# Out projection interleaved with the latent attention, 64-row scores and VectorE-released expert slots in a two-block transformer kernel

## The reference

```python
# block one, one layer
h, hc = rms_norm(x)*(1+mod1)+mod0, rms_norm(ctx)*(1+modc1)+modc0
qa, ka, va, qb, kb, vb, rb, gb, qn, kn, vn = split_in(h @ w_in)      # the same of hc
# ya: differential attention, 4 heads, softmax(q0 k0) - lam*softmax(q1 k1), 64 features each
# yb: gated linear attention; decay = log_sigmoid(gb @ w_dec + b_dec)/16, gb is 2 x 16 features
# yn: neighbourhood attention, 4 heads of 64 features
x = x + mod2 * (concat(ya, yb, yn) @ w_out)
x = x + mod5 * hier_moe(rms_norm(x)*(1+mod4)+mod3)
# block two, two layers
# ya: latent attention, 8 heads of 64+32 features, masked by chunks -> features 0..511
# yb: stick breaking attention, yc: pooling                         -> features 512..1023
x = x + concat(ya, yb, yc) @ w_out
x = x + hier_moe_2(rms_norm_2(x))        # top 2 of 32 experts, silu(h@gate)*(h@up) @ down
```

## Time and profile before

| what | value |
|---|---|
| median of 3 runs | 1709.47 us (1708.24 to 1713.54) |
| profiled execution, its own time | 1704.93 us |
| its span | 1703.1 us |
| TensorE busy | 1376.3 us (81%) |
| VectorE / ScalarE / GpSimd busy | 444.9 / 396.4 / 45.6 us |
| moved by DMA | 479.72 MB, mean 282 GB/s |
| mean granted TensorE clock | 0.92 of full speed |

### The profile page before, as it was taken

One profiled execution on the slowest core, in us unless ns is written; L12 is line 12 of the kernel. 1 busy time (PEld: TensorE's weight loads), 2 busy tenths in 40 slices (PEclk: granted clock), 3 DMA queues, 4 the chain that ended last, 5 costly groups with the idle time before them and its releaser, 6 DMA issues.

```text
span 1703.1 us, 31490 instructions
## 1 busy us (share of the span) xinstructions
PE 1376.3 (81%) x12314; PEld 726.0 (43%) x12315; DVE 444.9 (26%) x1355; ACT 396.4 (23%) x766; POOL 45.6 (3%) x85
## 2 busy tenths in 40 slices
PE   3899996879666776799969788977798887999775
PEld 2555463445333342355547444333337544444332
DVE  0102436642111111122233613211122524122112
ACT  1101214312111121122223411212122422222222
POOL 2000111100000000000000000000000000000000
PEclk9999968979989898899979889988899987999997
DMA  9968320168999999999893145999975314579994
GB/s 333 323 234 249 108 66 0 30 258 319 410 410 410 410 409 410 409 361 379 318 341 126 72 163 217 418 418 418 417 276 198 146 66 198 219 292 419 417 418 183
DMA packets 126112, 479.72 MB, mean 282 GB/s; under 512 B 9089, under 2 KB 19582, under 8 KB 109358
## 3 DMA queue, kind: packets, MB, share of 16 engines
q1 hardware_dynamic: 122496, 468.61, 70.3%
q0 software_dynamic: 2656, 8.81, 1.7%
q10 hardware_dynamic: 910, 1.59, 0.3%
HBM read 477.01 MB, written 1.97 MB: 281 GB/s over the span
## 4 chain that ended last, share of the span: by engine, by line
PE 54%; SPq 19%; DMA 12%; DVE 7%; issue 4%; ACT 2%; ACTq 0%; POOL 0%; DVEq 0%; PEldq 0%
SPq L489 19%; DMA store<-in_w_up 8%; PE psum L1037 6%; PE psum L1712 6%; PE psum L713 5%; PE psum L1014 4%; PE psum L1027 4%; PE psum L987 4%; PE psum L1048 3%; PE psum L1708 3%; PE psum L1055 2%; DMA store<-in_w_expert_down 2%; PE psum L1262 2%; PE psum L1274 2%; PE psum L593 1%
## 5 line engine op out<-in xcount | busy, mean ns | idle before, releaser
L1027 PE MATMUL psum<-store 128*32 128x256 f32 x2624 | 178.3, 412 | 69.6 <-DMA store<-in_w_expert_up 69.6
L1037 PE MATMUL psum<-store 128*32 128x256 f32 x2432 | 157.9, 417 | 41.9 <-DMA store<-in_w_up 41.7
L1179 DVE TENSOR_TENSOR store<-store,psum 128x128 f32<-128x128 f32 x79 | 22.7, 287 | 568.4 <-ACT store L1112 568.4
L1027 PEld LDWEIGHTS psum<-store 128*32 128x32 f32 x2624 | 78.9, 115 | 153.3 <-DMA store<-in_w_expert_up 101.6
L987 PE MATMUL psum<-xn,store 128*32 128x256 f32 (+1 forms) x992 | 129.5, 489 | 5.4 <-DVE store L1142 5.4
L1037 PEld LDWEIGHTS psum<-store 128*32 128x32 f32 x2432 | 92.3, 120 | 97.3 <-issue 64.8
L1014 PE MATMUL psum<-store 32*128 32x256 f32 (+1 forms) x992 | 128.6, 474 | 1.9 <-ACT store L1117 1.9
L1112 ACT ACT_TABLE_LOAD x79 | 101.4, 1283 | 49.0 <-issue 48.7
L1112 ACT ACTIVATE store<-psum 128x128 f32<-128x128 f32 x79 | 21.9, 277 | 342.0 <-PE psum L1027 192.2
L1712 PE MATMUL psum<-store 128*128 128x512 f32 x224 | 97.7, 593 | 0.0
L1014 PEld LDWEIGHTS psum<-store 32*128 32x128 f32 (+1 forms) x992 | 58.6, 190 | 75.5 <-issue 70.1
(11 more groups left out here) (324 smaller groups left out, 1505.3 us busy)
## 6 DMA issues: line engine op xcount, KB each, us to landing
store<-in_w_expert_up SPq DMA_DIRECT2D x128, 1024.0 KB, 18.3
store<-in_w_expert_down SPq DMA_DIRECT2D x64, 1024.0 KB, 18.4
store<-in_w_gate SPq DMA_DIRECT2D x64, 1024.0 KB, 18.8
store<-in_w_up SPq DMA_DIRECT2D x64, 1024.0 KB, 20.7
store<-in_w_down SPq DMA_DIRECT2D x64, 1024.0 KB, 22.1
store<-in_w_mod SPq DMA_DIRECT2D x12, 2048.0 KB, 14.7
store<-in_w_in SPq DMA_DIRECT2D x6, 2048.0 KB, 9.4
store<-in_w_out SPq DMA_DIRECT2D x6, 2048.0 KB, 16.7
```

The costliest lines, as they stand in the source:

```text
L1027: mm = pe.matmul(out_(j), chosen_rows(k, 0), wt[:, kk, :, j, :], start=(k == 0), stop=(k == KD - 1))
L1037: mm = pe.matmul(out_(j), chosen_rows(k, e), wt, start=(k == 0), stop=(k == KD - 1))
```

## The change

1. **Latent attention's banks** (`score_of`, `turned_of`, `values_of`). Both scores of an item share one bank (4 or 5), both transposes share bank 6, the values of even and odd pairs share bank 7. Banks 0 to 3 are free.
2. **Out projection in block two.** The 16 matmuls of j=1 are issued two at a time (`fill`) between the scores of i+2 and the transposes of i, for each of the 8 items; j=0 follows the attention. Block one keeps its order.
3. **64-row scores in block one.** The two score matmuls of an item read the 64 rows of head 2g and of head 2g+1 in place. `q_pad`, GpSimd's copies and `q_padded` are gone.
4. **Expert slots.** The first four slots of a round are counted in a new semaphore, `up_used`, which VectorE raises by 4 after `hid` of an expert's last round; TensorE raises `piece_used` by 2 for the two down slots at the end of the round. SP waits for the one or the other.
5. **`gb` and the decay inputs** are packed: four groups of 128 tokens in the four 32-column parts of the array, and then four groups of 32 rows. The small matrix `wdec` is loaded four times (8 DMAs on GpSimd's queue where 2 were). TensorE waits for 12 `mod_col` (VectorE) instead of 12 `mod_row` (ScalarE).

```diff
+UP = 4
+    def used(self, j):
+        return ("up_used", UP) if j < UP else ("piece_used", ROUND - UP)
+    def freed(self, r, j):
+        name, each = self.used(j)
+        return self.sems[name], self.base[name] + each * r + (j if j < UP else j - UP) + 1
...
-                        sp.wait_ge(sems["piece_used"], turn * RING + (stage.base + ROUND * i + j + 1))
+                        sem, count = stage.freed(i, j)
+                        sp.wait_ge(sem, turn * (TURN * stage.used(j)[1]) + count)
...
+        def score_of(kind, i):
+            if kind == "mla":
+                return ps[4 + i % 2].rearrange("p (m n) -> p m n", m=2)
+            return psum[:, 2 * (i % 2):2 * (i % 2) + 2, :]
+        def turned_of(kind, i, m):
+            if kind == "mla":
+                return ps[6][:, S * m:S * m + S]
+            return ps[4 + (i % 2 if kind == "diff" else m)]
+        def values_of(kind, g):
+            return ps[7][:, S * (g % 2):S * (g % 2) + S] if kind == "mla" else ps[6 + g % 2][:, 0:S]
...
-                if kind != "mla":
-                    pe.wait_ge(*at.plus("q_padded", i + 1))
...
-                        q, k = q_pad[:, i % 2, m, :], k_all[:, g, :]
+                        r = slice(64 * m, 64 * m + 64)
+                        q, k = (qnT if kind == "na" else qaT)[r, g, P * t:P * t + P], k_all[r, g, :]
...
-                if g >= 2:
-                    pe.wait_ge(*at.plus("pv_sb", g - 1))
+                lag = 1 if kind == "mla" else 2
+                if g >= lag:
+                    pe.wait_ge(*at.plus("pv_sb", g + 1 - lag))
...
                     scores(i + 2)
+                if fill:
+                    fill(i)
                 turns(i)
...
+        def out_steps_pe(pe, slot, j, first, last):
+            w = piece_at(slot, 4 * D).rearrange("p (k n) -> p k n", k=4)
+            for step in range(first, last):
+                t, n, k = step // 8, step // 4 % 2, step % 4
+                mm = pe.matmul(ps[2 * t + n], mixT[:, 4 * j + k, P * t:P * t + P], w[:, k, 512 * n:512 * n + 512],
+                               start=(j == 1 and k == 0), stop=(j == 0 and k == 3))
+                if step % 8 == 7:
                     mm.then_inc(sems["out_mm"], 1)
...
-                pe.sem_inc(sems["piece_used"], ROUND)
+                pe.sem_inc(sems["piece_used"], ROUND - UP)
...
                 dve.tensor_tensor(hid, silu_sb, U[:, P:2 * P], ALU.mult).then_inc(sems["w_hid"], 1)
+                if last:
+                    dve.sem_inc(sems["up_used"], UP)
...
-                attention_pe(pe, at, "mla")
-                out_projection_pe(pe, at, piece_ready, "wout2", mixT)
+                slot = piece_ready(("wout2", 1))
+                attention_pe(pe, at, "mla", fill=lambda i: out_steps_pe(pe, slot, 1, 2 * i, 2 * i + 2))
+                out_free_pe(pe, at)
+                out_rest_pe(pe, at, piece_ready, "wout2")
...
-                pool.dma_start(wdec[16 * d:16 * d + 16, d, :], ins["gla_w_decay"][0, d]).then_inc(sems["params2"], 16)
+                for g in range(4):
+                    o = 32 * g + 16 * d
+                    pool.dma_start(wdec[o:o + 16, d, :], ins["gla_w_decay"][0, d]).then_inc(sems["params2"], 16)
...
-            attention_pool(pool, at, "na")
-            attention_pool(pool, at, "diff")
...
-                        pe.wait_ge(sems["mod_row"], 12)
+                        pe.wait_ge(sems["mod_col"], 12)
                         for d in range(2):
-                            pe.matmul(ps[d], wdec[:, d, :], glow[0:32, :], start=True, stop=True).then_inc(sems["gate_z"], 1)
+                            for g in range(4):
+                                r = slice(32 * g, 32 * g + 32)
+                                mm = pe.matmul(ps[g][:, P * d:P * d + P], wdec[r, d, :], glow[r, 0:P], start=True, stop=True)
+                            mm.then_inc(sems["gate_z"], 1)
...
+                if what == "gb":
+                    for k in range(KD):
+                        for g in range(4):
+                            mm = pe.matmul(bank[32 * g:32 * g + 32, 0:P], w[:, k, 0:32], hT[:, k, P * g:P * g + P],
+                                           start=(k == 0), stop=(k == KD - 1))
```

More of the change, by code:

```diff
@@ L230, in place @@
         self.pos = (self.pos + 1) % (HOME // 2)
-        free = max(self.last[slot:slot + 2])
-        self.n += 2
-        self.last[slot:slot + 2] = [self.n, self.n]
+        free = self.last[slot + 1]
+        self.n["piece_used"] += 2
+        self.last[slot:slot + 2] = [("piece_used", self.n["piece_used"])] * 2
         self.loads[slot] += 16 * dmas
@@ L243, in stage @@
                 slot = stage.slot(r % TURN, j)
-                self.n += 1
-                self.last[slot] = self.n
+                name, _ = stage.used(j)
+                self.n[name] += 1
+                self.last[slot] = (name, self.n[name])
                 self.loads[slot] += 16
-        self.pos = 0 if self.last[0] < self.last[ROUND] else 3
+        self.pos = 0 if self.last[0][1] < self.last[ROUND][1] else 3
         return stage
@@ L495, in expert_loads @@
                 for j, src in enumerate(sources):
-                    sp.wait_ge(sems["piece_used"], max(stage.last[stage.slot(r, j)], 1))
+                    name, count = stage.last[stage.slot(r, j)]
+                    sp.wait_ge(sems[name], max(count, 1))
                     load(r, j, src[r])
@@ L506, in expert_loads @@
                 for j, src in enumerate(sources):
-                    sp.wait_ge(sems["piece_used"], stage.base + ROUND * (r - TURN) + j + 1)
+                    sp.wait_ge(*stage.freed(r - TURN, j))
                     load(r % TURN, j, src[r])
@@ L527, in keys_of, with attention_pe @@
             return P * (t + 1) if kind == "mla" else 4 * P
[L529 to L537, removed]
-                    ins_ = pool.tensor_copy(q_pad[r, i % 2, m, :], (qnT if kind == "na" else qaT)[r, g, P * t:P * t + P])
-                ins_.then_inc(sems["q_padded"], 1)
-            pool.wait_ge(*at("score", len(items)))
-        def attention_pe(pe, at, kind):
+        def score_of(kind, i):
[8 more added lines that the diff above has]
+            return ps[7][:, S * (g % 2):S * (g % 2) + S] if kind == "mla" else ps[6 + g % 2][:, 0:S]
+        def attention_pe(pe, at, kind, between=None, fill=None):
             items = items_of(kind)
@@ L645, in attention_act @@
             exps(1)
+            if between:
+                between(-1)
             for i in range(len(items)):
@@ L696, in attention_dve @@
                     maxima(i + 2)
+                if between:
+                    between(i)
                 if items[i][1] == NT - 1 and items[i][0] >= 1:
```

91 lines of the change are left out of this document (44 added, 47 removed).

## The result

| | before | after |
|---|---|---|
| median of the runs, us | 1708.93 (1708.24 to 1713.54, 4 runs) | 1661.09 (1655.85 to 1663.15, 4 runs) |
| profiled execution, its own time, us | 1704.93 | 1662.84 |
| its span, us | 1703.1 | 1661.0 |
| granted clock over the span | 0.920 | 0.919 |

The ratio is 0.971 [0.968, 0.974]: 47.8 us faster by the medians, where 34.2 us were forecast. The sign was right, the size was not. The two profiled executions differ by 42.1 us. Before's lay 4.0 us under its median and after's 1.75 us above, which makes up the 5.7 us between 42.1 and 47.8.

The account below looks back on a forecast made before the run. Weight loads were taken to pace part of each expert stage, TensorE's chain the out projection. Terms 6.4 + 5.2 + 15.2 + 7.4 = 34.2 us gave 1670.7 us profiled, 1675.3 us median; range 1666 to 1690 us.

Parts of the forecast that it names:

- part 4: Block two's latent attention: j=1 matmuls between the items let j=0 start earlier; 3.7 us per layer, 7.4 in both.
- part 1: Packed `gb` and decay inputs on TensorE: 5.2 and 1.5 us saved, less a 0.3 us wait; net 6.4 us.
- part 2: 64-row scores in block one's attentions: score pairs take half their time, shortening VectorE's waits; 5.2 us.
- part 3: Expert stages: up slots given back by VectorE after `hid` start the weight stream earlier; 3.8 + 5.7 + 5.7 = 15.2 us.
- That idle time remains: Latent attention: TensorE's idle time at 954 to 960 us stays, so 3.4 us per layer goes to 1.2 GHz.
- the sum of durations: Latent attention, item 2's scores to j=0: 27.19 us of groups and fills plus waits, so j=0 starts 7.1 us earlier.
- full clock in the latent attention: Rival: gapless TensorE work is granted 2.4 GHz throughout, fills give 14.2 us, total 1668.5 us; chance 0.12.
- The reference point: Whole kernel: profiled execution forecast at 1670.7 us, median at 1675.3, since before's profiled execution lay 4.5 us under its median.
- the edge of what I allowed: Block one's scores: an item's pair takes 0.5 to 0.6 of its time; half was taken, 0.6 would give 4.6 us.
- The 0.3 us allowed for the semaphore and the queue: Expert stages: delay between the end of `hid` and the first awaited load, some 0.3 us taken off each stage's gain.

Follow-up runs that it names:

- alone, by the ratio: Kernel before with only that row's part applied; in the order of the rows 1701.41, 1702.71, 1690.7 and 1688.81 us.
- spare fills: Changed kernel with the 16 j=1 matmuls between items as throwaway work and all 16 again after the attention: 1682.87 us, ratio 0.9852 to before.
- part 4 alone: Kernel before with only the latent attention's packed banks and j=1 fills in block two: 1688.81 us, ratio 0.9886 to before.

## Why the prediction was wrong in size

**What it got right.** The direction and, outside part 4, the mechanisms. Terms against the profiled pair:

| term, us | forecast | profiled pair | alone, by the ratio |
|---|---|---|---|
| part 1 | 6.4 | 5.8 | 8.4 |
| part 2 | 5.2 | 1.8 | 6.7 |
| part 3 | 15.2 | 16.0 | 18 |
| part 4 | 7.4 | 15.9 | 19.5 |
| not forecast | 0 | 2.6 | |
| sum | 34.2 | 42.1 | 52.6 |

For part 3 the pair's figure is the shift of the three first awaited loads, 3.9 + 6.1 + 6.1 us with rounding; by the stages' lengths it is 3.0 + 7.5 + 5.9. The line "not forecast" is what is left: 0.8 us before anything changed had run, 3.1 in the GLA, -1.7 in layer two's dense part, and small pieces. The 3.1 are an accident of one execution: in its second trace the same kernel had 35.01 us there.

**The step that failed is in part 4**: "That idle time remains, so I leave the same stretch at 1.2 GHz: 3.4 us. Per layer 7.1 - 3.4 = 3.7". In layer one j=0 starts 35.76 - 26.20 = 9.56 us earlier. 9.56 = 3.7, plus the 3.4 that the clock didn't take, plus 2.5 that I lost in the sum of durations: 27.19 + 0.75 + 0.74 = 28.68 us was summed where 26.20 passed. Each of the 18 groups other than the fills overlaps with its neighbour by some 0.16 us. Against it j=0 itself took 1.7 us longer in the profiled execution.

The kernel without fills settles the whole at 20.3 us, and the one with spare fills shows that the clock is a cause and not a companion: more work, no row at 1.2 GHz, a clock of 1.00 instead of 0.71. The rival "full clock in the latent attention" (chance 0.12, 14.2 us) is what happened, and it was still too small by the overlap: 14.2 + 2 x 2.5 = 19.2 us. I named it and gave it too little. The 3.4 us was too small a price for the clock even as a term: it was taken from 10 us at 0.66, while the whole stretch of 21.48 us stood at 0.76 and had lost 5.2.

The Trainium skill, TensorE: Matmul & The Clock Gate, Part 1, says that activity releases the throttle. By that rule the traces agree (1.00 in the filled stretch, 0.76 in the same stretch before).

The idle time that I took for the reason, at 954 to 960 in before, indeed remains (TensorE is busy for 3.90 of those 6 us in both traces), but the attention behind it had the full clock in the changed kernel, with part 4 alone and with spare fills.

**The reference point was off too.** I set the forecast for the median 4.54 us above that for the profiled execution. Before's profiled execution was a quick one; after's was 1.75 us slower than its median. Of the 14.2 us between forecast and measurement 6.3 are this. The other 7.9 are the terms: part 4 alone 8.5, while the rest, -3.4 in part 2 and +2.6 not forecast among them, nearly cancel. The 6.3 us are the chance of two single executions, and not of the mechanism.

**Part 2** has the right mechanism: 1.88 became 1.13 us, 0.6 of it, at the edge of what I allowed. Its size changed from trace to trace: 1.8 us in the changed kernel's, 3.9 alone, 6.7 to 9 by the ratios. All kernels with 128-row scores have 68.4 to 68.7 us there at a clock of 0.90 to 0.93. Of those with 64-row scores and no fills in block one, five traces have 66.7 to 66.9 us at 0.85, and three 64.5 to 64.6 at 0.87 to 0.89. So 1.5 to 4.2 us are seen in these attentions, and the rest of the 6.7 to 9 isn't placed. Less TensorE work there left it more idle, and a lower clock went with it. That the first caused the second was not tested.

**Part 3** came out as worked out: loads 4, 6 and 6 us earlier, the stream of the same length behind them. The 0.3 us allowed for the semaphore and the queue weren't taken: the load goes 0.23 us after the start of `hid`, which is 0.06 before its end, and that is most of the difference between 15.2 and 16.0. What VectorE's extra instruction costs by itself no run shows.

**Part 1** came out at 5.8: 5.1 us from `gb` and the rest from the decay inputs behind their 0.35 us wait. The 8.4 us that it gave alone go beyond that, and the excess isn't placed.

**What stays open.** How much idle time lets the clock down was not tried. Why the unchanged GLA takes about 32, 33.5 or 35 us isn't explained; the clock goes with it. Over the whole GLA it is 0.56 in the traces with 35 us (before's, and the changed kernel's second), 0.59 in one with 33.6, and 0.63 in those with 32. What decides between them, and between the two lengths of j=0, is not known; one kernel can show either. The 10 us that fills in front cost are placed only to 5.4.

## What to carry to other kernels

Where an edit fills TensorE's gaps with work that was due anyway, price the filled stretch at full clock, and let the time that the old stretch lost to 1.2 GHz count as a gain. The work behind it may still come out slow (15.67 us for 13.97 in the changed kernel). Count from start to start, not by sums of durations: over eighteen short groups the sum was 2.5 us too long. In a stage that weights pace, an earlier release is worth what the first awaited load moves forward (here to within 1.5 us in each stage of the profiled pair), and a forecast for a median should not rest on where a single profiled execution lay.

## What the runs showed of the hardware

- 14 us of extra TensorE work in the attention's gaps cost 4.0 and 4.3 us there, at a granted clock of 1.00 instead of 0.71 and 0.76. The matmuls behind ran 2.2 us quicker in layer one and no quicker in layer two.
- With fills in the first half of the attention only, waits of 1.93 us for VectorE were back in the second half, and the granted clock of the stretch stayed at 1.00.
- The same 32 records of 128 x 512 took 13.97, 15.67, 16.21 or 16.97 us. The gap in front doesn't settle it: with part 4 alone j=0 took 13.97 us behind a gap of 1.00 us in layer one, and 15.67 behind 0.99 in layer two, and the changed kernel's two traces differ in just this.
- A pair of 64-row scores on different row groups takes 0.6 of the time of a 128-row pair and not half (1.13 against 1.88 us), and four-fold packing of 32 columns took `gb` from 7.03 to 1.95 us, 3.6 times quicker.
- The GLA, whose code was the same in all kernels, took 31.9 to 35.1 us; two executions of the changed kernel took 31.97 and 35.01.
